# Gate-up chunks of three feed-forwards as seven quarter products over sums of quarters, tiles in three parts with own down products

## The chip, the cores and the metric

One core of one Trainium2 chip. The time is that of the program on the device in microseconds, taken as the median over runs; lower is better. TensorE is called PE, VectorE DVE, ScalarE ACT, GpSimd POOL, SyncE SP, as in the profile.

## What is computed

The program is two blocks of a language model over 512 tokens with 1024 features, in 32-bit floats: pooling, sparse attention and a short convolution in the first (with 16 more tokens ahead), two kinds of attention in the second, and three feed-forwards. Only these matter here:

```python
gate, up = jnp.split(hn @ w_gate_up, 2, axis=-1)
h = h + (jax.nn.silu(gate) * up) @ w_down
...
x = x + 0.5 * swiglu(rms_norm_2(x, ffn1_norm[i]), ffn1_w_gate[i], ffn1_w_up[i], ffn1_w_down[i])
...
x = x + 0.5 * swiglu(rms_norm_2(x, ffn2_norm[i]), ffn2_w_gate[i], ffn2_w_up[i], ffn2_w_down[i])
```

Each has 2816 hidden features, which are 22 tiles of 128 (`FK`).

## The kernel before

The residual `hT` lies transposed in SBUF: eight tiles (k = 0 to 7) of 128 features by 16 + 512 tokens. Weights come in numbered chunks of 128 x 2048 floats (1 MB, two transfers of 512 KB). A chunk c goes through four stages, with two buffers each, chosen by c % 2:

- SP loads it into `raw` (`load`, line 394), once POOL is done with chunk c - 2.
- ACT rounds it to PE's 32-bit format into `whi` (`high`, line 1206) once PE is done with chunk c - 2.
- POOL subtracts, `wlo = raw - whi`, in four parts (`low`, line 566).
- PE multiplies. A product of full precision is three passes: high weights by high activations, high by low, low by high (`passes`, lines 693 to 695). `chunk` makes two output tiles (t = 0, 1) of 128 x 512 tokens, each over eight k: 48 matmuls of 512 columns. The outputs lie in two of eight PSUM banks, chosen by c % 2, and PE waits on `acc_free` until they have been read.

In a feed-forward (f = 0, 1, 2, each engine has its function `ffn`) the chunks C_F[f] + n hold gate tile n and up tile n. PE sums the squares during the first chunk, ACT takes the root, DVE the reciprocal `rs` (line 1705), which ends during the second chunk. In the second feed-forward two norms follow each other, and DVE and ACT take turns twice (`closing_root`). For tile n DVE scales gate and up by `rs` into `tmp` (line 1736), ACT takes the silu (line 1251), DVE multiplies (line 1761), ACT rounds the product to `fh` (line 1253), DVE makes its low part `fl` (line 1764). ACT's order for tile n is: `high` of chunk n + 2, silu of tile n, rounding of tile n.

When all 22 tiles are there, 12 down chunks follow: four blocks of 256 output features, each in three chunks of 8, 8 and 6 tiles of k that add up in one PSUM bank, so that DVE adds a block to `hT` once, after its third chunk (`update`). Each finished tile is fed on (`feed`): ACT scales and rounds it to `xh` and squares it, DVE makes `xl` and adds the squares, for the next stage. In the second feed-forward DVE scales the eight tiles of `hT` (line 1677 of the profile) ahead of its down chunks.

The order of work is the order of each engine's code: engines run theirs strictly in turn and wait on semaphores. Gate-up and down chunks were loops on every engine; the second attention's chunks are written out.

## Time and profile before

| | |
|---|---|
| median of 3 runs | 1999.79 us (1999.69 to 2000.12) |
| span of the profiled execution | 1998.1 us |
| the profiled execution's own time | not given apart; the median has 1.7 us around the span |
| PE busy | 1990.9 us, 9505 matmuls |
| POOL, DVE, ACT busy | 1007.5, 877.9, 732.3 us |
| feed-forwards in the span | about 487 to 846, 846 to 1219 and 1580 to 1938 us |
| mean HBM traffic | 92 GB/s |

The profile has one execution. Busy time of PE is modelled and overlaps, so that the distance between starts is the price of a matmul, not its duration. A wait is put down to what ended it.

### The profile page before, as it was taken

What the parts mean: (1) busy time and instruction counts of PE and PEld (TensorE: products, weight loads), DVE (VectorE), ACT (ScalarE), POOL (GpSimd) and SP (SyncE); (2) the same over time, 40 slices, a digit from 0 to 9 for tenths busy, and PEclk for the clock granted to TensorE, in tenths of its full rate; (3) what the DMA queues carried; (4) which work ended last, traced back from release to release, by engine and by line L of the source; (5) the groups of instructions that cost most, each with busy time, mean ns of one, the idle gap of its engine ahead of it and who ended that gap; (6) DMA issues with size and microseconds to landing.
All of it is one profiled execution on the core that took longest, in us unless ns stands there. A gap on an engine that the chain in (4) does not pass through costs nothing.

```text
span 1998.1 us, 26696 instructions
## 1 busy us (share of the span) xinstructions
PE 1990.9 (100%) x9505; PEld 1668.7 (84%) x9505; DVE 877.9 (44%) x1467; ACT 732.3 (37%) x1034; POOL 1007.5 (50%) x795
## 2 busy tenths in 40 slices
PE   9999999999999999999999999999999999999999
PEld 8998887788888888888888888889888888888887
DVE  6587756535333322153334115677645523332124
ACT  6413234444222323232232225667643422322232
POOL 5444442245555544455555446565654555555443
PEclk9999999999999999999999999999999999999999
DMA  5233231133333332333332232332222333332332
GB/s 179 87 92 99 85 104 43 49 100 93 96 105 86 103 100 80 109 90 105 85 104 90 98 107 85 109 103 75 72 87 85 104 105 84 105 95 89 98 107 85
DMA packets 253787, 188.81 MB, mean 94 GB/s; under 512 B 6608, under 2 KB 249680, under 8 KB 253680
## 3 DMA queue, kind: packets, MB, share of 16 engines
q1 hardware_dynamic: 253024, 187.53, 31.5%
q8 instruction: 44, 0.72, 0.2%
q10 hardware_dynamic: 688, 0.31, 0.1%
q14 instruction: 31, 0.25, 0.0%
HBM read 180.93 MB, written 2.10 MB: 92 GB/s over the span
## 4 chain that ended last, share of the span: by engine, by line
PE 98%; ACT 1%; DVE 1%; issue 0%; DMA 0%; SPq 0%; ACTq 0%; DVEq 0%
PE ps L693 30%; PE ps L695 30%; PE ps L694 30%; PE ps L989 1%; PE ps L1141 1%; PE ps L1061 1%; PE ps L1062 1%; PE ps L1063 1%; PE ps L1129 1%; PE ps L1128 0%; PE ps L983 0%; PE ps L1111 0%; PE ps L1099 0%; PE ps L882 0%; PE ps L1098 0%
## 5 line engine op out<-in xcount | busy, mean ns | idle before, releaser
L566 POOL TENSOR_TENSOR wlo<-raw,whi 128x512 fp32r<-128x512 f32 (+2 forms) x636 | 852.9, 1373 | 862.1 <-ACT whi L1206 773.1
L693 PE MATMUL ps<-xh,whi 128*128 128x512 f32 (+1 forms) x1872 | 716.1, 383 | 0.0
L695 PE MATMUL ps<-xh,wlo 128*128 128x512 f32 (+1 forms) x1872 | 709.0, 379 | 0.0
L694 PE MATMUL ps<-xl,whi 128*128 128x512 f32 (+1 forms) x1872 | 708.7, 379 | 0.0
L1206 ACT ACTIVATE whi<-raw 128x2048 fp32r<-128x2048 f32 (+1 forms) x149 | 280.1, 1880 | 765.0 <-PE ps L695 764.9
L695 PEld LDWEIGHTS ps<-xh,wlo 128*128 128x128 f32 x1872 | 351.5, 188 | 66.8
L693 PEld LDWEIGHTS ps<-xh,whi 128*128 128x128 f32 x1872 | 351.7, 188 | 64.4 <-issue 0.7
L694 PEld LDWEIGHTS ps<-xl,whi 128*128 128x128 f32 x1872 | 352.0, 188 | 62.1 <-issue 0.7
L1736 DVE TENSOR_TENSOR tmp<-ps,rs 128x512 f32<-128x512 f32 x148 | 101.9, 691 | 313.1 <-PE ps L695 295.6
L695 PE MATMUL ps<-fh,wlo 128*128 128x512 f32 x528 | 205.4, 389 | 0.0
L693 PE MATMUL ps<-fh,whi 128*128 128x512 f32 x528 | 205.4, 389 | 0.0
L694 PE MATMUL ps<-fl,whi 128*128 128x512 f32 x528 | 205.4, 389 | 0.0
L1677 DVE SCALAR_TENSOR_TENSOR hT<-ps,hT 128x512 f32 x40 | 27.6, 690 | 270.6 <-PE ps L695 269.6
L1761 DVE TENSOR_TENSOR tmp<-tmp 128x512 f32<-128x512 f32 x66 | 90.3, 1369 | 111.9 <-ACT tmp L1251 111.7
L693 PEld LDWEIGHTS ps<-fh,whi 128*128 128x128 f32 x528 | 99.1, 188 | 20.7
L694 PEld LDWEIGHTS ps<-fl,whi 128*128 128x128 f32 x528 | 99.1, 188 | 20.6
L695 PEld LDWEIGHTS ps<-fh,wlo 128*128 128x128 f32 x528 | 99.1, 188 | 20.5
L644 POOL TENSOR_TENSOR wlo<-raw,whi 128x384 fp32r<-128x384 f32 (+1 forms) x84 | 75.6, 931 | 51.3 <-ACT whi L1572 50.6
L1211 ACT ACTIVATE xh<-hT,vec (+1 forms) x48 | 34.9, 727 | 127.2 <-DVE hT L1677 125.7
L1253 ACT ACTIVATE fh<-tmp 128x512 f32 x66 | 41.8, 633 | 102.4 <-DVE tmp L1761 102.4
L1764 DVE TENSOR_TENSOR fl<-tmp,fh 128x512 f32 x66 | 51.2, 775 | 62.3 <-ACT fh L1253 62.3
L1677 DVE SCALAR_TENSOR_TENSOR xl<-hT,vec,xh (+1 forms) x48 | 46.0, 960 | 57.5 <-ACT xh L1211 57.4
(335 smaller groups left out, 2247.1 us busy)
## 6 DMA issues: line engine op xcount, KB each, us to landing
raw<-in_w_in SPq DMA_DIRECT2D x87, 512.0 KB, 4.6
raw<-in_w_gate_up SPq DMA_DIRECT2D x44, 512.0 KB, 4.7
raw<-in_ffn_w_gate SPq DMA_DIRECT2D x44, 512.0 KB, 4.0
raw<-in_ffn_w_up SPq DMA_DIRECT2D x44, 512.0 KB, 5.2
raw<-in_ffn_w_down SPq DMA_DIRECT2D x32, 512.0 KB, 4.0
raw<-in_w_down SPq DMA_DIRECT2D x16, 512.0 KB, 4.0
raw<-in_ffn_w_down SPq DMA_DIRECT2D x16, 384.0 KB, 3.6
raw<-in_w_b SPq DMA_DIRECT2D x8, 512.0 KB, 4.0
```

The lines of the kernel that those rows point to most:

```text
L566: ins = pool.tensor_tensor(wlo[:, c % 2, cs], raw[:, c % 2, cs], whi[:, c % 2, cs].bitcast(F32), ALU.subtract)
L644: ins = pool.tensor_tensor(wlo[:, c % 2, cs], raw[:, c % 2, cs], whi[:, c % 2, cs].bitcast(F32), ALU.subtract)
L693: pe.matmul(o, w_of(whi), xhi, start=first, stop=False)
L694: pe.matmul(o, w_of(whi), xlo, start=False, stop=False)
L695: return pe.matmul(o, w_of(wlo), xhi, start=False, stop=last)
L1206: act.activation(whi[:, c % 2, 0:n], raw[:, c % 2, 0:n], ACT.Copy).then_inc(w_hi, 1)
L1211: act.activation(one(xh, nn)[:, lo:TM], one(hT, nn)[:, lo:TM], ACT.Copy, scale=col(vec, lin(gain + n, per, i))).then_inc(xh_done, 1)
L1253: act.activation(one(fh, lin(n, per, i)), tmp[:, 3, :], ACT.Copy).then_inc(h_hi, 1)
L1677: return dve.scalar_tensor_tensor(o, a, s, b, op0, op1)
L1736: dve.tensor_tensor(o, ps[0:o.shape[0], bank(c, t), :], rsx[0:o.shape[0]], ALU.mult).then_inc(acc_free, 1)
L1761: dve.tensor_tensor(tmp[:, 3, :], tmp[:, 1, :], tmp[:, 2, :], ALU.mult).then_inc(h_done, 1)
L1764: dve.tensor_tensor(one(fl, nn), tmp[:, 3, :], one(fh, nn).bitcast(F32), ALU.subtract).then_inc(h_split, 1)
```

## The change

Of the 22 tiles of a feed-forward, 18 (tiles 4 to 21) are *folded*. The weights of a chunk are taken as four corners (k 0 to 3 or 4 to 7, gate or up) of 512 x 128, and the tokens as two halves, early and late, of 256. Instead of eight products of a corner with a quarter of the activations, each engine's code makes seven, over sums of corners and sums of activation quarters (the scheme of Strassen and Winograd): 7 x 4 k x 3 passes = 84 matmuls of 256 columns. Sums of weights: DVE forms three in PSUM (`corner_sums`), ACT rounds them, DVE makes their low parts (`sums_low`); POOL forms the fourth (`low_sum`) and the low parts of three corners. Sums of activations (`fold_forms`, `fold_sums`: "forms" below, numbers 0 to 3) are made once per feed-forward, by ACT and DVE together, number 0 at place 0, numbers 1 and 2 at place 1, number 3 at place 2. Three partial products are copied out of PSUM by ACT (`kept`) and added by DVE; PE goes on with the bank when the copy is made. The low part of an activation moves from DVE to POOL (`act_low`).

A feed-forward has 34 *places* p, chunk C_F[f] + p: 7 up tiles, 4 down chunks over tiles 0 to 5, 8 up tiles, 4 down chunks over tiles 6 to 13, 7 up tiles, 4 down chunks over tiles 14 to 21. `fh` and `fl` are rings of nine tiles. Each down chunk has its own PSUM bank per half and is added to `hT` by DVE in two steps. Silu and product of a tile now run at the place after it. All loops of the feed-forwards are written out. Some semaphores are merged and buffers moved, in stages that stay as they are.

Core of the diff (`corner_sums`, `sums_low` and `act_low` are told above):

```diff
-DOWN_K = (8, 8, 6)
+DOWN_K = (6, 8, 8)
+UPS = (7, 8, 7)
+PLAIN = 4
+RING = 9
+FOLD = CW
...
+FORMS_AT = {0: (0,), 1: (1, 2), 2: (3,)}
...
+            def fold_low(f, p):
+                c, n = C_F[f] + p, fold_no(f, p)
+                for z, (a, b) in enumerate(((0, 0), (1, 1), (1, 0))):
+                    hi, lo = unit(c, z)
+                    if z == 2:
+                        pool.wait_ge(w_lo, c)
+                        pool.tensor_tensor(low_sum[:], corner(c, 1, 1), corner(c, 0, 1), ALU.subtract).then_inc(corner_low, 1)
+                    pool.wait_ge(raw_hi, 3 * n + z + 1)
+                    pool.tensor_tensor(by_k(lo), corner(c, a, b), by_k(hi).bitcast(F32), ALU.subtract).then_inc(raw_lo, 1)
+                if up_tile(p - 2) is not None:
+                    act_low(f, p - 2)
+                hi, lo = unit(c, 3)
+                pool.wait_ge(w_hi, c + 1)
+                pool.tensor_tensor(by_k(lo), low_sum[:], by_k(hi).bitcast(F32), ALU.subtract).then_inc(w_lo, 1)
...
+            def ffn(f):
+                low(C_F[f])
+                low(C_F[f] + 1)
+                for p in range(1, FFN_LEN):
+                    if folded(p + 1):
+                        fold_low(f, p + 1)
+                        continue
+                    if down_part(p) is not None and up_tile(p - 1) is not None:
+                        act_low(f, p - 1)
+                    if p + 1 < FFN_LEN:
+                        low(C_F[f] + p + 1)
+                    if down_part(p) is None and up_tile(p - 1) is not None:
+                        act_low(f, p - 1)
...
+                pe.wait_ge(raw_lo, 3 * n + 1)
+                pe.wait_ge(acc_free, 2 * (c - 2) + 2)
+                product(r1, 0, xh[:, k1, late], xl[:, k1, late]).then_inc(prod_done, 1)
+                if n % (FK - PLAIN) == 0:
+                    pe.wait_ge(fs_lo, 8 * f + 8)
+                pe.wait_ge(sum_lo, 3 * n + 1)
+                product(r5, 4, *forms(0)).then_inc(prod_done, 1)
+                pe.wait_ge(sum_lo, 3 * n + 2)
+                pe.wait_ge(prod_kept, 3 * n + 1)
+                product(r1, 5, *forms(2), first=False).then_inc(prod_done, 1)
+                pe.wait_ge(raw_lo, 3 * n + 2)
+                pe.wait_ge(prod_kept, 3 * n + 2)
+                product(r5, 1, *forms(3), first=False).then_inc(prod_done, 1)
+                pe.wait_ge(w_lo, c + 1)
+                pe.wait_ge(prod_kept, 3 * n + 3)
+                product(r1, 3, *forms(1), first=False).then_inc(prod_done, 1)
+                pe.wait_ge(raw_lo, 3 * n + 3)
+                pe.wait_ge(up_done, 2 * n + 1)
+                product(r2, 2, xh[:, k2, late], xl[:, k2, late]).then_inc(tile_done, 1)
+                pe.wait_ge(sum_lo, 3 * n + 3)
+                pe.wait_ge(up_done, 2 * n + 2)
+                product(r1, 6, xh[:, k2, early], xl[:, k2, early], first=False).then_inc(tile_done, 1)
...
+                pe.wait_ge(w_lo, c + 1)
+                for t in range(2):
+                    pe.wait_ge(acc_free, 2 * (c - 2) + t + 1)
+                    for k in range(DOWN_K[r]):
+                        if j == 0 and t == 0:
+                            pe.wait_ge(h_split, FK * f + k0 + k + 1)
+                        o, z = CW * k + P * t, (k0 + k) % RING
+                        mm = passes(ps[:, bank(c, t), :], c % 2, lambda wt: wt[:, c % 2, o:o + P],
+                                    fh[:, z, :], fl[:, z, :], k == 0, k == DOWN_K[r] - 1)
+                    mm.then_inc(tile_done, 1)
...
-                def up(c, n, per=0, i=None):
-                    high(c + 2, per, i)
-                    act.wait_ge(acc_free, lin(2 * c + 1, 2 * per, i))
-                    act.activation(tmp[:, 1, :], tmp[:, 0, :], ACT.Silu).then_inc(silu_done, 1)
-                    act.wait_ge(h_done, lin(FK * f + n + 1, per, i))
-                    act.activation(one(fh, lin(n, per, i)), tmp[:, 3, :], ACT.Copy).then_inc(h_hi, 1)
...
+            def fold_high(f, p, z):
+                c, n = C_F[f] + p, fold_no(f, p)
+                def corner_high(u, a, b):
+                    act.activation(by_k(unit(c, u)[0]), corner(c, a, b), ACT.Copy).then_inc(raw_hi, 1)
+                def sum_high(u, m):
+                    act.wait_ge(corner_sum, 3 * n + min(m + 2, 3))
+                    act.activation(unit(c, u)[0], ps[:, 3 + 2 * m, :], ACT.Copy).then_inc(sum_hi, 1)
+                if z == 0:
+                    act.wait_ge(raw_in[c % 2], raw_level(c, 0, None))
+                    if n:
+                        act.wait_ge(corner_sum, 3 * n - 2)
+                    act.activation(sums(1), corner(c, 0, 1), ACT.Copy).then_inc(corner_in, 1)
+                    act.wait_ge(tile_done, 2 * (c - 1))
+                    corner_high(0, 0, 0)
+                elif z == 1:
+                    corner_high(1, 1, 1)
+                    sum_high(4, 0)
+                elif z == 2:
+                    sum_high(5, 1)
+                else:
+                    corner_high(2, 1, 0)
+                    sum_high(6, 2)
+                    act.wait_ge(corner_low, n + 1)
+                    act.activation(by_k(unit(c, 3)[0]), low_sum[:], ACT.Copy).then_inc(w_hi, 1)
...
+            def fold_forms(f, i, gain):
+                for z, n in enumerate((i, i + 4)):
+                    ins = act.activation(ps[:, 1, FOLD * z:FOLD * z + FOLD], hT[:, n, META:META + FOLD], ACT.Copy,
+                                         scale=vec[:, gain + n:gain + n + 1])
+                ins.then_inc(fs_in, 1)
+                for z in range(2):
+                    act.wait_ge(fs_sum, 2 * (4 * f + i) + z + 1)
+                    act.activation(fsh[:, 2 * z:2 * z + 2, i, :], ps[:, 5 + 2 * z, :].rearrange("p (y t) -> p y t", y=2),
+                                   ACT.Copy).then_inc(fs_hi, 1)
...
+                act.wait_ge(rt_done, S + 1)
+                for p in range(FFN_LEN):
+                    c, n = C_F[f] + p, up_tile(p - 1)
+                    def coming(z):
+                        if folded(p + 1):
+                            fold_high(f, p + 1, z)
+                        elif folded(p):
+                            high_piece(c + 1, z)
+                        elif p and z == 0:
+                            high(c + 1)
+                    def kept(dst, src, level):
+                        if folded(p):
+                            act.wait_ge(prod_done, 5 * fold_no(f, p) + level)
+                            act.activation(dst[:], src, ACT.Copy).then_inc(prod_kept, 1)
+                    r1, r5, _ = fold_out(c)
+                    if n is not None and not folded(p - 1):
+                        act.wait_ge(acc_free, 2 * (c - 1) + 1)
+                        act.activation(tmp[:, 1, :], tmp[:, 0, :], ACT.Silu).then_inc(silu_done, 1)
+                    for i in FORMS_AT.get(p, ()):
+                        fold_forms(f, i, own)
+                    coming(0)
+                    if folded(p - 1):
+                        act.wait_ge(acc_free, 2 * c)
+                        act.activation(tmp[:, 1, :], tmp[:, 0, :], ACT.Silu).then_inc(silu_done, 1)
+                    kept(prod1, r1, 1)
+                    coming(1)
+                    kept(prod5, r5, 2)
+                    coming(2)
+                    if n is not None:
+                        act.wait_ge(h_done, FK * f + n + 1)
+                        act.activation(fh[:, n % RING, :], tmp[:, 3, :], ACT.Copy).then_inc(h_hi, 1)
+                    kept(prod6, r1, 3)
+                    coming(3)
...
+            def fold_sums(f, i, own):
+                a, b = slice(0, FOLD), slice(FOLD, T)
+                early, late = slice(META, META + FOLD), slice(META + FOLD, TM)
+                x, s13, s24 = ps[:, 1, :], ps[:, 5, :], ps[:, 7, :]
+                g1, g2 = (vec[:, own + n:own + n + 1] for n in (i, i + 4))
+                dve.wait_ge(fs_in, 4 * f + i + 1)
+                if f or i:
+                    dve.wait_ge(fs_lo, 2 * (4 * f + i))
+                link(stt(s13[:, a], hT[:, i, early], g1, x[:, b], ALU.mult, ALU.add))
+                stt(s13[:, b], hT[:, i, late], g1, x[:, a], ALU.mult, ALU.subtract)
+                stt(s24[:, a], hT[:, i, late], g1, s13[:, a], ALU.mult, ALU.subtract).then_inc(fs_sum, 1)
+                dve.wait_ge(fs_sum, 2 * (4 * f + i) + 1)
+                stt(s24[:, b], hT[:, i + 4, late], g2, s24[:, a], ALU.mult, ALU.add).then_inc(fs_sum, 1)
+                for z, s in enumerate((s13, s24)):
+                    dve.wait_ge(fs_hi, 2 * (4 * f + i) + z + 1)
+                    dve.tensor_tensor(fsl[:, 2 * z:2 * z + 2, i, :], s.rearrange("p (y t) -> p y t", y=2),
+                                      fsh[:, 2 * z:2 * z + 2, i, :].bitcast(F32), ALU.subtract).then_inc(fs_lo, 1)
...
+                for p in range(FFN_LEN):
+                    c, n, last = C_F[f] + p, up_tile(p - 1), FK * f + (up_tile(p - 1) or 0)
+                    new = folded(p + 1)
+                    if folded(p - 1):
+                        done(c - 1, 1)
+                        dve.tensor_tensor(tmp[:, 0, 0:FOLD], fold_out(c - 1)[0], rsx[:, 0:FOLD], ALU.mult).then_inc(acc_free, 1)
+                    if new:
+                        corner_sums(f, p + 1, 0)
+                        corner_sums(f, p + 1, 1)
+                    if n is not None:
+                        dve.wait_ge(silu_done, last + 1)
+                        if last:
+                            dve.wait_ge(h_split, last)
+                        if folded(p - 1):
+                            dve.wait_ge(up_done, 2 * fold_no(f, p - 1) + 2)
+                            dve.tensor_tensor(tmp[:, 3, :], tmp[:, 1, :], tmp[:, 2, :], ALU.mult).then_inc(h_done, 1)
+                        else:
+                            done(c - 1, 1)
+                            link(dve.tensor_tensor(tmp[:, 3, :], tmp[:, 1, :], ps[:, bank(c - 1, 1), :], ALU.mult))
+                            dve.sem_inc(acc_free, 1)
+                            dve.sem_inc(h_done, 1)
+                    for i in FORMS_AT.get(p, ()):
+                        fold_sums(f, i, own)
+                    if new:
+                        corner_sums(f, p + 1, 2)
+                        sums_low(f, p + 1, 0)
+                        sums_low(f, p + 1, 1)
+                    if folded(p):
+                        m = fold_no(f, p)
+                        r1, r5, r2 = fold_out(c)
+                        dve.wait_ge(prod_done, 5 * m + 4)
+                        dve.wait_ge(prod_kept, 3 * m + 3)
+                        dve.wait_ge(h_done, FK * f + up_tile(p))
+                        dve.tensor_tensor(tmp[:, 2, FOLD:T], r5, prod6[:], ALU.add).then_inc(up_done, 1)
...
+                        stt(tmp[:, 2, :], ps[:, bank(c, t), :], factor, rsx, ALU.mult, ALU.mult).then_inc(acc_free, 1)
+                        dve.wait_ge(acc_free, 2 * c + t + 1)
+                        dve.tensor_tensor(x, x, tmp[:, 2, :], ALU.add).then_inc(h_new, 1)
```

## Rows read from the trace of the kernel before

**Rows 1.** The page: busy time and share of each engine; the chain that ended last, by engine.
```profile
PE 1990.9 (100%) x9505; PEld 1668.7 (84%) x9505; DVE 877.9 (44%) x1467; ACT 732.3 (37%) x1034; POOL 1007.5 (50%) x795
...
PE 98%; ACT 1%; DVE 1%; issue 0%; DMA 0%; SPq 0%; ACTq 0%; DVEq 0%
```

**Rows 2.** Timeline at the third gate-up chunk: start us, duration us, engine, line, operation.
```profile
508.65 0.39 PE L693 MATMUL ps<-xh,whi 128*128 128x512 f32 x1
...
508.85 1.92 ACT L1206 ACTIVATE whi<-raw 128x2048 fp32r<-128x2048 f32 x1 [4.74 <-PE ps L695]
...
519.73 1.92 ACT L1206 ACTIVATE whi<-raw 128x2048 fp32r<-128x2048 f32 x1 [6.28 <-PE ps L695]
```

**Rows 3.** Timeline of PE in a value chunk with 256 columns.
```profile
1363.75 0.28 PE L1061 MATMUL ps<-whi,xh 128*128 128x256 f32 x1
...
1364.71 0.28 PE L1063 MATMUL ps<-whi,xl 128*128 128x256 f32 x1
```

**Rows 4.** Matmuls of the output projection's first pass: duration ns min/median/max, first and last start.
```profile
L693 PE MATMUL ps<-mh,whi x64: 389/389/389, 442.9 to 485.8; 128*128 128x512 f32 x64
```

**Rows 5.** Groups of ACT and DVE by shape: count, busy us, mean ns, idle before.
```profile
L1253 ACT ACTIVATE fh<-tmp 128x512 f32 x66 | 41.8, 633 | 102.4 <-DVE tmp L1761 102.4
...
L1416 ACT ACTIVATE fpTh<-ps 128x256 fp32r<-128x256 f32 x16 | 6.2, 384 | 17.8 <-PE ps L1129 17.7
...
L1736 DVE TENSOR_TENSOR tmp<-ps,rs 128x512 f32<-128x512 f32 x148 | 101.9, 691 | 313.1 <-PE ps L695 295.6 <-DVE fl L1764 12.5 <-DVE rs L1705 0.4
L1761 DVE TENSOR_TENSOR tmp<-tmp 128x512 f32<-128x512 f32 x66 | 90.3, 1369 | 111.9 <-ACT tmp L1251 111.7
...
L2174 DVE TENSOR_TENSOR fpTl<-ps,fpTh 128x256 fp32r<-128x256 f32 x16 | 6.8, 422 | 5.4 <-ACT fpTh L1416 5.3
```

**Rows 6.** Groups of POOL by shape.
```profile
L566 POOL TENSOR_TENSOR wlo<-raw,whi 128x512 fp32r<-128x512 f32 x556 | 781.9, 1438 | 752.9 <-ACT whi L1206 735.5 <-ACT whi L1346 17.4
...
L566 POOL TENSOR_TENSOR wlo<-raw,whi 128x384 fp32r<-128x384 f32 x48 | 47.4, 1021 | 37.6 <-ACT whi L1206 37.6
```

**Rows 7.** Timeline of POOL: one part beside a DVE op, one alone.
```profile
512.10 1.74 POOL L566 TENSOR_TENSOR wlo<-raw,whi 128x512 fp32r<-128x512 f32 x1
...
1593.30 1.29 POOL L566 TENSOR_TENSOR wlo<-raw,whi 128x512 fp32r<-128x512 f32 x1 [3.80 <-ACT whi L1206]
```

**Rows 8.** Timeline at the start of the first feed-forward: ACT's rounding, DVE after the root.
```profile
497.97 1.92 ACT L1206 ACTIVATE whi<-raw 128x2048 fp32r<-128x2048 f32 x1
...
500.19 1.29 DVE L1736 TENSOR_TENSOR tmp<-ps,rs 128x512 f32<-128x512 f32 x2 [0.22 <-DVE rs L1705]
```

**Rows 9.** The same at the second and third feed-forward.
```profile
863.04 1.72 DVE L1724 TENSOR_TENSOR rs<-rs,ssum 128x512 f32<-128x512 f32 x1
864.98 1.29 DVE L1736 TENSOR_TENSOR tmp<-ps,rs 128x512 f32<-128x512 f32 x2 [0.22 <-DVE rs L1724]
...
869.71 1.92 ACT L1206 ACTIVATE whi<-raw 128x2048 fp32r<-128x2048 f32 x1 [1.24 <-PE ps L695]
...
1591.30 1.92 ACT L1206 ACTIVATE whi<-raw 128x2048 fp32r<-128x2048 f32 x1 [1.41 <-PE ps L695]
...
1592.20 1.29 DVE L1736 TENSOR_TENSOR tmp<-ps,rs 128x512 f32<-128x512 f32 x2 [0.22 <-DVE rs L1705]
```

**Rows 10.** Timeline of PE at the start of the kernel.
```profile
1.07 4.51 PE L743 MATMUL ps<-ones 128*128 128x512 f32 x10 [1.07 <-DVE eps L1801]
```

**Rows 11.** Timeline of DVE: the eight scalings ahead of the second down stage.
```profile
1093.07 7.15 DVE L1677 SCALAR_TENSOR_TENSOR hT<-hT,vec,ssum 128x512 f32<-128x512 f32 x8 [0.22 <-DVE fl L1764]
```

**Rows 12.** Timeline of POOL and DVE at the last chunk of a projection.
```profile
1573.40 5.49 POOL L566 TENSOR_TENSOR wlo<-raw,whi 128x512 fp32r<-128x512 f32 x4 [5.47 <-ACT whi L1206]
...
1580.12 0.69 DVE L1677 SCALAR_TENSOR_TENSOR hT<-ps,hT 128x512 f32 x1 [0.68 <-PE ps L695]
```

**Rows 13.** Page, DMA issues: count, KB each, us to landing.
```profile
raw<-in_ffn_w_up SPq DMA_DIRECT2D x44, 512.0 KB, 5.2
```

**Rows 14.** Busy time of each engine in the unrolled attention stage, granted clock, DMA.
```profile
1280.00:1492.00 212.00, 211.36 (x1177) 183.34 (x1176) 136.26 (x306) 133.24 (x299) 123.09 (x123) 1.00 0.33 95
```

More of the change, by code:

```diff
@@ L322, in n_cols @@
                 return DK * (P + KW)
[L323 to L326 removed]
+            part = down_part(ffn_place(c)[1])
+            return CH if part is None else DOWN_K[part[0]] * CW
         def value_tile(c, t, z):
```

341 lines of the change are left out of this document (203 added, 138 removed).

## Prediction

> **What bounds the kernel now.** I read the page's busy times first, then the chain that ended last, then the timeline of single chunks. TensorE (PE) is busy for 1990.9 of 1998.1 us, and the chain is PE for 98% [rows 1]: what shortens the work of PE shortens the kernel, as long as nothing else makes PE wait. The stretch of the feed-forwards has the shape to remember. ScalarE (ACT) starts its rounding of a weight chunk 0.20 us after PE begins the chunk before it (508.65 to 508.85), and the next one comes 10.88 us later [rows 2]. So one gate-up chunk is 48 matmuls of 512 columns at 0.2267 us, with no hole. Behind it run ACT (1.92 us to round), then POOL (four low parts, 5.2 to 5.9 us): some 8 us of each 10.88. That chain is hidden, but it has under 3 us to spare: an ACT that comes to its rounding late shows at once.
>
> **1. The seven products.** A folded chunk issues 7 products x 4 k x 3 passes = 84 matmuls of 256 columns. The nearest rows are the value chunks with 256 columns: eight steps in 0.96 us, 0.120 us each [rows 3]. 84 x 0.120 = 10.08 against 10.88 us: 0.80 us less. 54 chunks are folded (18 in each of three feed-forwards): **-43.2 us**. The bounds: half of 0.2267 (0.113 us) would give 1.36 us a chunk, -73; 0.122 us, -34. I take the row, which has the shape itself. The 12 waits within a chunk cost nothing once they are met: the output projection waits ahead of each of its k, and its 64 first passes, three matmuls apart, take 42.9 us, 0.681 a step, three times 0.227 [rows 4].
> The Trainium skill (TensorE: Matmul & The Clock Gate, section Back-to-back issue gap) has a smaller fixed part per matmul, 2.5 ns beside the columns; by it the chunks would be 10.36 and 9.17 us and the term -64. Rows 2 and 3 give more than that at both widths, and the rows decide.
>
> **2. The steady folded chunk.** What is prepared for the next chunk while PE works on this one, in us from PE's start, with 0.19 for PE's last result to reach another engine: ACT has eight copies of 512 (six halves and sums rounded, one corner into PSUM, one sum of POOL's), three of 256, a silu and a rounding: 10 x 0.63 + 3 x 0.38 = 7.4 of 10.08. DVE has six of 512 with a PSUM operand, five of 256 and the product of the silu: 6 x 0.69 + 5 x 0.42 + 1.37 = 7.6. POOL has six of 512 (before four; the activation's low part moves to it): 8.6 at the mean of 1.438, 7.7 at the 1.29 of an undisturbed one [rows 5 to 7]. All fit. The tightest hand-off is the third product, which ACT must copy out (0.38) before PE's fifth writes there at 5.76. Ahead of it ACT has a corner (to 0.82), the silu (1.34), the first copy (2.05), a corner and a sum (3.1), the second copy (3.5), the second sum, which waits for DVE's third corner sum (4.15), and the rounding of the activation (4.7); the copy ends at 5.0. Slack 0.75: nothing is paid. The fifth product's sum on DVE ends at 7.8, needed at 8.64. **0 us**, with up to 0.1 late (5 us in all) if no ACT copy overlapped the next and DVE's product took its full 1.37.
>
> **3. The start of each feed-forward.** This is where I expect the loss. Chunk 2 (the third) needs its weights rounded by ACT. Before, ACT did that ahead of the silu, at 497.97, right after the table load [rows 8]. Now ACT's order at place 1 is: silu of tile 0, forms 1, forms 2, and only then the rounding of chunk 2. The silu waits for DVE's scaling of tile 0, which stands behind the root (its reciprocal; tmp is written from 500.19 [rows 8]) and behind forms 0. From the root's end R, with 0.04 a hand-off:
> - forms 0: four 256-wide sums on DVE, 0.42 each with hand-offs between (1.85), ACT's copy of the last (0.63), DVE's low part (0.69): the scaling starts at R + 3.3
> - scaling 0.69, silu 0.63, product 0.69: R + 5.4
> - forms 1: 1.85 + 0.63, and ACT's two scaled halves for forms 2 (0.75): R + 8.7; forms 2: 1.85 + 0.63: R + 11.2
> - rounding 1.92, started 0.1 before the copy's end as ACT's ops do, four parts on POOL at 1.29: **R + 18.2**.
> R is 500.19; PE wants chunk 2 at 508.65 [rows 2]: it waits 9.7 us. In the second feed-forward R was 864.98, of which 1.03 is a product that ran 1.72 instead of 0.69 beside POOL, which now stands still; chunk 2 was due 0.20 before 869.71: 863.95 + 18.2 - 869.51 = 12.6. In the third, R 1592.20, due at 1591.10 + 10.88 = 1601.98: 8.4 [rows 9]. Sum **+30.8**. The bounds: 0.69 for each of the 12 narrow sums adds 12 x 0.27 x 3 = +10; if they overlap throughout and the POOL parts follow faster, -9.
> **The clock.** After such a wait PE may come back at its lower level. The only row of that is the kernel's start: ten 512-column matmuls take 4.51 us, 0.45 apart and not 0.227, while the column of the granted clock shows full speed there too; 2.2 us are lost [rows 10]. Without it, chunk 3 would come 0.7 late in its turn (forms 3 stand ahead of its rounding, 4.5 + 1.9 + 5.2 = 11.6 from the start of chunk 2, against 10.88). One takes the place of the other: 0.7 to 2.2, I take 2.2 as the one with a row. **+6.6**.
>
> **4. From up to down.** The chunk after the last up tile is rounded in four pieces between ACT's other copies, the last ending at 5.5, and POOL's four parts end at 10.7 where PE wants them at 10.08: +0.65 in parts 1 and 2. In part 0 the down chunk has six k, POOL takes 4 x 1.02 and is in time [rows 6], but then the low part of tile 6 stands ahead of the next chunk's on POOL: ready at 8.9 after the first down chunk's start, wanted at 8.16: +0.75. Tile 21 is wanted 21 matmuls (4.76) into its down chunk and is ready 5.4 after the up chunk, 4.75 into it: nothing. 2.05 a feed-forward; in the second the eight scalings of the residual (7.15 us on DVE, two operands in SBUF each [rows 11]) now fall beside POOL's work for part 0: five POOL ops, slowed by some 0.35 each (an undisturbed one takes 1.29, the disturbed one of rows 7 1.74), 1.7 more. **+7.9**.
>
> **5. Down products alone.** Matmuls are the same in number. Each of 36 chunks has its own evacuation, per half one DVE pass from PSUM and one add: 4 us of 8.16 or more, covered by the next chunk, as PSUM has two sets. In the last part ACT's rounding stands behind the feed, 0.7 later than in the output projection, where POOL's four parts end at 1578.89 and the next chunk starts 0.19 before 1580.12, 1.04 later [rows 12]: 0.3 is left, covered; 0.3 is lost before the second feed-forward's sums of squares. **+0.3**. SP's loads are the same in number and size; a slot is freed at 9.5, filled 5.2 us later [rows 13] at 4.6 of the next chunk, and wanted at 6.5. Unrolled code: in the stretch that is unrolled now, PE stood 0.64 of 212 us [rows 14]; 0 to 3 us for the feed-forwards, taken as 0.
>
> **Sum.** -43.2 + 30.8 + 6.6 + 7.9 + 0.3 = +2.4 on a span of 1998.1; with the 1.7 us that the median of the runs (1999.8) has around it: **2002.2 us**.
>
> **The rivals.**
> (a) *The start is covered* (DVE and ACT get through the forms so early that chunk 2 is in time, or I have the order of waits wrong): the terms of 3 go, 2002.2 - 37.4 = 1965. For: ACT stands idle for most of the first chunks. Against: it stands idle waiting for the root, and so would the forms. In between, each microsecond off the chain R + 18.2 is 3 us.
> (b) *POOL becomes the bound*, slower than before. Six subtractions at 1.74 us, as the row of one that met a DVE op with two SBUF inputs [rows 7], are 10.44 us; over 10.08 by 0.36, times 54 is 19.4: 2021. It decides once the six, with POOL's waits for ACT (about 1.3 us), pass 10.08, that is from 1.46 us each. For: their mean in the feed-forwards is 1.438. Against: DVE now has one op a chunk with two SBUF inputs instead of two, since the sums lie in PSUM. The Trainium skill (SBUF — State Buffer, section Who interferes with whom) says that only such DVE ops hold GpSimd up. By that rule five of six run at 1.29, and this rival falls; the rows of 1.29 and 1.74 bear it out.
> (c) *The 256-column matmuls run at a worse pitch in this mix*: at 0.125 the 54 chunks take 84 x 0.005 x 54 = 23 us more: 2025. Against: rows 3.
>
> **How the numbers follow.** My case, 0.60, lies from 1990 to 2013 (chain -9 to +10, clock -4.5, code +3). (a) with its halfway forms 0.18, (b) 0.15, (c) 0.07. The range 1983 to 2021 leaves out most of (a) and the worst of (b) and (c). 0.2% is 4.0 us, about what a measurement of this kernel tells from no change: faster (below 1995.8) is (a) and the low fifth of my case, 0.32; slower (above 2003.8) is (b), (c) and a good third of mine, 0.42; the rest 0.26.
>
> **What would show it.** A folded chunk 10.08 us apart in the timeline. PE idle once per feed-forward ahead of chunk 2 for 8 to 13 us, released by POOL's low part, with ACT's copies of the forms before its rounding; matmuls 0.43 apart after it. Idle of about 0.7 before down chunks. I am wrong in step 2 if PE waits for ACT's copies within folded chunks, and in step 3 if PE runs through.

## The result, and the profile after

The changed kernel takes **2016.94 us** (median of 4 runs, 2016.16 to 2017.48), the kernel before 1999.82 beside it: 1.0085 times as long, 95% interval 1.0071 to 1.0099. It is slower by 17.1 us, and by more than the 2.4 us forecast; it lies inside the range of 1983 to 2021, but above the 1990 to 2013 of my own case. The profiled execution took 2016.82 us with a span of 2015.0.

The page of the changed kernel: busy times, the granted clock in 40 slices of the span, the chain by engine, and, by shape, two groups of POOL.

```profile
PE 1962.6 (97%) x11449; PEld 1731.6 (86%) x11449; DVE 1189.4 (59%) x2067; ACT 937.5 (47%) x1649; POOL 1123.3 (56%) x915
...
PEclk9999999999899999989999999999999989999999
...
PE 86%; DVE 4%; POOL 4%; ACT 4%; issue 2%; DMA 0%; SPq 0%; DVEq 0%; ACTq 0%
...
L631 POOL TENSOR_TENSOR wlo<-raw,whi 128x512 fp32r<-128x512 f32 x340 | 462.9, 1393 | 470.0 <-ACT whi L1350 414.9 <-ACT whi L1395 37.7 <-ACT whi L1561 17.5
...
L654 POOL TENSOR_TENSOR wlo<-raw,whi 128x512 fp32r<-128x512 f32 x162 | 212.9, 1316 | 160.1 <-ACT whi L1404 160.1
```

Beside [rows 1], PE's work has shrunk and the span has grown. The chain, 98% PE before, now leaves PE for a seventh of the span: something makes PE wait. POOL, the second rival's suspect, is no busier than 56%, and its subtractions of 512 columns have become shorter: 1.393 us, and 1.316 in the folded chunks, where 1.438 stood in [rows 6]. The clock column has a dip in slices 11, 18 and 33, where the feed-forwards begin. The list of PE's waits (us in total, how many, the longest) says who ends them:

```profile
PE ps L793 <- POOL wlo L631: 40.8, 15, 12.7
PE ps L944 <- ACT prod L1461: 4.7, 6, 0.8
```

For a ledger I took, from 480 us on, every distance from the start of a matmul of 512 or 256 columns to the next start, and subtracted what the shape takes undisturbed: 0.2267 us for 512 columns [rows 2], 0.120 for 256 [rows 3]. What is left over, called lost below, adds up to 6.7 us before and 67.2 after. So 60.5 us are lost and 43.2 won, which is the 17. Where the clock stays full, a loss is 0.2 to 0.3 us more than the idle time in brackets, since the first matmuls behind a wait are further apart. Where they are lost:

| place | f = 0 | f = 1 | f = 2 | sum | forecast |
|---|---|---|---|---|---|
| ahead of chunk 2, slow clock included | 12.84 | 14.70 | 10.54 | 38.1 | 37.4 |
| ahead of the second down chunk of part 0 | 1.33 | 4.70 | 1.33 | 7.4 | 4.0 |
| ahead of the first down chunk of parts 1 and 2 | 1.26 | 1.26 | 1.25 | 3.8 | 3.9 |
| ahead of the fourth product of the first folded chunk of parts 1 and 2 | 2.04 | 2.02 | 2.04 | 6.1 | 0 |
| chunks of the last part's feed | 3.73 | 0.1 | 0.1 | 3.9 | 0.3 |

The folded chunks themselves run as fast as forecast. PE at the first chunk and at the end of the third of a row:

```profile
543.00 0.28 PE L944 MATMUL ps<-xh,whi 128*128 128x256 f32 x1
543.11 0.28 PE L945 MATMUL ps<-xl,whi 128*128 128x256 f32 x1
...
573.11 0.28 PE L946 MATMUL ps<-xh,foldl 128*128 128x256 f32 x1
573.23 0.40 PE L793 MATMUL ps<-fh,whi 128*128 128x512 f32 x1
```

From 543.00 to 573.23 are three chunks of 84 matmuls, 30.23 us: 10.08 each.

The start of the first feed-forward, PE (in brackets the idle time before an instruction, and who ended it):

```profile
508.15 0.39 PE L795 MATMUL ps<-xh,wlo 128*128 128x512 f32 x1
518.28 0.79 PE L793 MATMUL ps<-xh,whi 128*128 128x512 f32 x1 [9.74 <-POOL wlo L631]
518.87 0.63 PE L794 MATMUL ps<-xl,whi 128*128 128x512 f32 x1
519.30 0.63 PE L795 MATMUL ps<-xh,wlo 128*128 128x512 f32 x1
...
523.99 0.57 PE L794 MATMUL ps<-xl,whi 128*128 128x512 f32 x1
524.39 0.39 PE L795 MATMUL ps<-xh,wlo 128*128 128x512 f32 x1
```

And ACT there:

```profile
501.17 1.12 ACT L1436 ACTIVATE fsh<-ps 128x512 fp32r<-128x512 f32 x2 [2.67 <-DVE ps L1892]
503.73 0.63 ACT L1466 ACTIVATE tmp<-tmp 128x512 f32<-128x512 f32 x1 [1.43 <-DVE tmp L2057]
504.26 0.86 ACT L1431 ACTIVATE ps<-hT,vec 128x256 f32<-128x256 f32 x2
506.83 1.12 ACT L1436 ACTIVATE fsh<-ps 128x512 fp32r<-128x512 f32 x2 [1.72 <-DVE ps L1892]
507.85 0.87 ACT L1431 ACTIVATE ps<-hT,vec 128x256 f32<-128x256 f32 x2
510.30 1.12 ACT L1436 ACTIVATE fsh<-ps 128x512 fp32r<-128x512 f32 x2 [1.57 <-DVE ps L1892]
511.32 1.90 ACT L1350 ACTIVATE whi<-raw 128x2048 fp32r<-128x2048 f32 x1
```

PE stands 9.74 us for POOL, and POOL began its four parts at 513.30, when ACT had rounded. ACT rounds at 511.32, behind the silu (503.73), forms 1 and forms 2; before, it did that ahead of the silu [rows 8]. In between it stands idle three times for DVE (1.43, 1.72, 1.57 us), with the rounding ready to run. After the wait, matmuls start 0.427 us apart.

### The profile page after: what moved, and what is told of

It is laid out like the page before. It is cut to its first block, busy times and chain, and to the rows that moved or that the text cites. A ratio compares the mean times of both kernels' runs of the same rounds, so it can differ in the third digit from the quotient of the medians.

```text
span 2015.0 us, 30682 instructions
## 1 busy us (share of the span) xinstructions
PE 1962.6 (97%) x11449; PEld 1731.6 (86%) x11449; DVE 1189.4 (59%) x2067; ACT 937.5 (47%) x1649; POOL 1123.3 (56%) x915
## 3 DMA queue, kind: packets, MB, share of 16 engines
q8 instruction: 87, 1.43, 0.3%
## 4 chain that ended last, share of the span: by engine, by line
PE 86%; DVE 4%; POOL 4%; ACT 4%; issue 2%; DMA 0%; SPq 0%; DVEq 0%; ACTq 0%
PE ps L793 18%; PE ps L794 18%; PE ps L795 18%; PE ps L944 8%; PE ps L946 8%; PE ps L945 8%; POOL wlo L631 4%; PE ps L1133 1%; PE ps L1285 1%; ACT whi L1350 1%; DVE ps L1892 1%; PE ps L1205 1%; PE ps L1206 1%; PE ps L1207 1%; DVE tmp L1892 1%
## 5 line engine op out<-in xcount | busy, mean ns | idle before, releaser
L631 POOL TENSOR_TENSOR wlo<-raw,whi 128x512 fp32r<-128x512 f32 (+2 forms) x420 | 537.5, 1312 | 579.1 <-ACT whi L1350 433.9
L793 PE MATMUL ps<-xh,whi 128*128 128x512 f32 (+1 forms) x1008 | 383.5, 380 | 31.7 <-POOL wlo L631 31.7
L794 PE MATMUL ps<-xl,whi 128*128 128x512 f32 (+1 forms) x1008 | 375.2, 372 | 0.0
L795 PE MATMUL ps<-xh,wlo 128*128 128x512 f32 (+1 forms) x1008 | 375.1, 372 | 0.0
L654 POOL TENSOR_TENSOR wlo<-raw,whi 128x512 fp32r<-128x512 f32 x162 | 212.9, 1316 | 160.1 <-ACT whi L1404 160.1
L793 PEld LDWEIGHTS ps<-xh,whi 128*128 128x128 f32 x1008 | 191.2, 190 | 65.0 <-POOL wlo L631 33.8
L795 PEld LDWEIGHTS ps<-xh,wlo 128*128 128x128 f32 x1008 | 190.8, 189 | 33.7
L794 PEld LDWEIGHTS ps<-xl,whi 128*128 128x128 f32 x1008 | 191.5, 190 | 28.9 <-issue 0.7
L944 PE MATMUL ps<-fsh,whi 128*128 128x256 f32 x432 | 122.7, 284 | 4.7 <-ACT prod L1461 4.7
L946 PE MATMUL ps<-xh,wlo 128*128 128x256 f32 x432 | 122.3, 283 | 0.0
```

The lines of the kernel that those rows point to most:

```text
L631: ins = pool.tensor_tensor(wlo[:, c % 2, cs], raw[:, c % 2, cs], whi[:, c % 2, cs].bitcast(F32), ALU.subtract)
L654: pool.tensor_tensor(by_k(lo), corner(c, a, b), by_k(hi).bitcast(F32), ALU.subtract).then_inc(raw_lo, 1)
L793: pe.matmul(o, w_of(whi), xhi, start=first, stop=False)
L794: pe.matmul(o, w_of(whi), xlo, start=False, stop=False)
L795: return pe.matmul(o, w_of(wlo), xhi, start=False, stop=last)
L944: pe.matmul(o, wh[:, ks], hi[:, k, :], start=first and k == 0, stop=False, skip_group_check=True)
```

## The experiments

Each kernel is the changed one with one thing altered; the last ones put several together. Times beside 2016.94. The start in the wanted order and the last two kernels were run 4, 5 and 5 times, each of the others once.

### ACT rounds before it makes the forms

```diff
+                    coming(0)
                     for i in FORMS_AT.get(p, ()):
                         fold_forms(f, i, own)
-                    coming(0)
```

> ACT rounds the next chunk's weights ahead of the forms at places 1 and 2, nothing else is changed. Theory (the rounding of chunk 2 waits in ACT's order behind forms 1 and 2, and POOL and PE with it): the rounding of chunk 2 starts some 6.5 us earlier, right behind the silu of tile 0, and the three waits of 9.7, 12.7 and 8.4 us ahead of chunk 2 shrink by 6 to 7 us each, to about 3, 6 and 2. With the clock's loss unchanged the kernel takes 1995 to 1998 us, and 1990 where the clock no longer falls. First rival (DVE's reciprocal and forms, not ACT's order, set the start): the waits stay within 1 us of what they were, 2015 us or more. Second rival (the forms are wanted just as much): as much is lost again ahead of chunk 4, the first folded one, by PE waiting for the low parts of the forms, and the time stays at 2012 or more.

Measured: 1991.53 us. One line moved, 25.4 us less. The list of PE's waits:

```profile
PE ps L793 <- POOL wlo L631: 19.7, 15, 5.6
```

21.1 us of waits are gone (40.8 to 19.7), and the three starts lose 3.0, 7.4 and 1.7 us in the ledger. The first rival falls: DVE's forms are as they were. So does the second: no new wait for the forms. In the second feed-forward the clock still falls; the 1995 to 1998 and the 1990 of the theory were for all three places or none, and it came out between.

### Forms 2 one place later

```diff
-    FORMS_AT = {0: (0,), 1: (1, 2), 2: (3,)}
+    FORMS_AT = {0: (0,), 1: (1,), 2: (2, 3)}
```

> Forms 2 are made at place 2 together with forms 3, in place of place 1. Theory (ACT's order, and one op of it is worth what it takes): the wait ahead of chunk 2 is shorter by what forms 2 take, 2.5 to 2.9 us in each feed-forward; forms 2 and 3 then stand ahead of the rounding of chunk 3, behind a product of DVE's that waits for POOL's low part of tile 0, and chunk 3 comes 2 to 4 us late in its turn. The sum is within 4 us of 2016.8. Rival (forms 2 have room at place 2): the first wait is shorter and none appears, 2008 us.

Measured: 2013.21 us. PE's idle times ahead of chunk 2 are 6.28, 9.18 and 4.97 us, each 3.5 shorter, not 2.5 to 2.9: forms 2 take ACT from 507.85 to 511.32 above, 3.5. With the slow clock behind them the starts lose 8.0, 11.6 and 6.8 us, 11.7 less in all. And chunk 3 is late by 4.5, 2.2 and 2.7 us, 9.4 together. The wait moves, as expected: what stands ahead of a rounding is paid at one chunk or at the next. Of the 3.7 us that the kernel is faster, 1.6 lie elsewhere: at the second down chunk of part 0 in the second feed-forward PE stands the same 2.83 us, but the clock does not fall behind it, and 3.1 us are lost and not 4.7.

### PE kept busy through the wait

```diff
+                        if p == 2:
+                            for _ in range((40, 52, 34)[f]):
+                                pe.matmul(ps[:, 3, :], ones[:], xh[:, 0, META:TM], start=True, stop=True)
                         chunk(c + p, xh, xl)
```

> PE makes 40, 52 and 34 matmuls of 512 columns with no use ahead of chunk 2 of the three feed-forwards (9.1, 11.8 and 7.7 us at 0.227 each, a little less than its waits there), into a PSUM bank that holds nothing at that time. Theory (the 0.43 us from one matmul to the next behind the wait come from PE having stood still): with them the matmuls of chunk 2 are 0.227 apart from the first on, the remaining wait is under 1 us in each, and 6 to 8 us are won: 2009 to 2011 us. The granted clock's half level is gone from these three places. Rival (the slow matmuls come from chunk 2's own data or from POOL and ACT beside them): the pitch behind the wait stays at 0.43 and the time at 2016 to 2018.

Measured: 2013.52 us, 3.4 less and not 6 to 8. PE where the useless matmuls end and chunk 2 begins:

```profile
516.17 1.29 PE L1002 MATMUL ps<-xh,ones 128*128 128x512 f32 x5
518.26 0.50 PE L793 MATMUL ps<-xh,whi 128*128 128x512 f32 x1 [0.79 <-POOL wlo L631]
518.59 0.40 PE L794 MATMUL ps<-xl,whi 128*128 128x512 f32 x1
518.83 0.39 PE L795 MATMUL ps<-xh,wlo 128*128 128x512 f32 x1
```

The mechanism is as the theory has it: the first two distances are 0.33 and 0.24, then 0.23, and the three starts, with 28.6 us of useless matmuls counted as wait, lose 32.0 in place of 38.1. So the slow clock costs 6.1 us at the three starts. But now chunk 3 is late: 0.93, 0.93 and 0.85 us, 2.7 together. While PE was slow, POOL caught up. Net 3.4, which is the difference in time. The prediction had this ("Without it, chunk 3 would come 0.7 late in its turn"); my expectation for this run had forgotten it.

### ACT's start in the order in which it is wanted

```diff
 # fold_forms, between its scalings and its copies
+                if i == 0:
+                    high(C_F[f] + 2)
 # ffn: the first two tiles rounded ahead of the forms, chunk 3 after forms 1
+                    if p in (1, 2):
+                        act.wait_ge(h_done, FK * f + n + 1)
+                        act.activation(fh[:, n % RING, :], tmp[:, 3, :], ACT.Copy).then_inc(h_hi, 1)
                     for i in FORMS_AT.get(p, ()):
                         fold_forms(f, i, own)
+                        if i == 1:
+                            high(C_F[f] + 3)
```

> ACT's work at the start of a feed-forward is put in the order in which it is wanted: it rounds chunk 2 right after its first two scalings for forms 0, while DVE makes them; chunk 3 after forms 1; and the products of tiles 0 and 1 ahead of the forms of their places. Theory (all 38 us lost at the three starts, clock included, come from ACT's order): the waits ahead of chunks 2 go to under 1.5 us in the first and third feed-forward and under 3 in the second, none larger than 1 us comes ahead of chunks 3 and 4, and the kernel takes 1978 to 1985 us, faster than the kernel before. First rival (only the order is changed, and DVE's forms are late for chunk 4 instead): a wait of 3 us or more for the forms ahead of its second product, 1990 or more. Second rival (the loss is spread over all folded chunks and not at the starts): 2005 or more.

Measured: **1983.72 us** (1983.34 to 1984.75), 0.992 times the kernel before, interval 0.9903 to 0.9936. ACT at the start:

```profile
498.72 0.88 ACT L1431 ACTIVATE ps<-hT,vec 128x256 f32<-128x256 f32 x2
499.53 1.90 ACT L1350 ACTIVATE whi<-raw 128x2048 fp32r<-128x2048 f32 x1
502.27 1.12 ACT L1438 ACTIVATE fsh<-ps 128x512 fp32r<-128x512 f32 x2 [0.83 <-DVE ps L1899]
```

The rounding fits into the 2.67 us for which ACT stood idle ahead of 501.17. In the first and third feed-forward the starts lose nothing at chunks 2 and 3, and 0.5 and 0.2 us at the first folded chunk. In the second they lose 4.1 there:

```profile
889.66 0.28 PE L946 MATMUL ps<-fsh,foldl 128*128 128x256 f32 x1
892.38 0.55 PE L944 MATMUL ps<-fsh,foldh 128*128 128x256 f32 x1 [2.44 <-ACT prod L1463]
892.73 0.42 PE L945 MATMUL ps<-fsl,foldh 128*128 128x256 f32 x1
```

That is more than the theory's 1 us ahead of chunk 4, and it is the first rival's place, though for a product's copy and not for the forms. The root comes later there, two norms in a row [rows 9]: the forms begin 5.7 us before PE starts chunk 2 (859.38 and 865.12), in the first feed-forward 8.6 (500.83 and 509.47), and all that follows them is late.

### POOL's order at the first down chunk

```diff
-                    if down_part(p) is not None and up_tile(p - 1) is not None:
+                    if down_part(p) == (2, 0):
                         act_low(f, p - 1)
                     if p + 1 < FFN_LEN:
                         low(C_F[f] + p + 1)
-                    if down_part(p) is None and up_tile(p - 1) is not None:
+                    if down_part(p) != (2, 0) and up_tile(p - 1) is not None:
                         act_low(f, p - 1)
 # PE's down_chunk
-                    pe.wait_ge(acc_free, 2 * (c - 2) + t + 1)
+                    pe.wait_ge(acc_free, 2 * (c - 2) + (2 if folded(p - 2) else t + 1))
```

> POOL makes the low part of the last up tile of parts 0 and 1 (which the down products of the part don't use) behind the four low parts of the next down chunk, not ahead of them; PE's first half of the second down chunk waits for both halves of the folded chunk before. Theory (the second down chunk of part 0 is late by the one POOL op that stands ahead of its low parts): PE's losses there, 1.33, 4.70 and 1.33 us after the change, go to 0.1, under 1.5 and 0.1, and the kernel takes 2009 to 2011 us. The losses of 0.63 ahead of the first down chunk of parts 1 and 2 stay. Rival (POOL is late by the residual's scalings beside it in the second feed-forward, not by its order): the 1.33 go and of the 4.70 at least 2.5 stay, 2011 to 2014. Second rival (ACT's rounding is late, not POOL's part): nothing moves, 2016 to 2018.

Measured: 2010.89 us, 6.0 less. The losses of 1.33, 4.70 and 1.33 us are gone, the second one whole. POOL in the changed kernel in the first feed-forward, and below in the second:

```profile
576.96 1.29 POOL L643 TENSOR_TENSOR fl<-tmp,fh 128x512 fp32r<-128x512 f32 x1 [3.24 <-ACT fh L1479]
578.21 4.37 POOL L631 TENSOR_TENSOR wlo<-raw,whi 128x384 fp32r<-128x384 f32 x4
...
946.83 1.73 POOL L643 TENSOR_TENSOR fl<-tmp,fh 128x512 fp32r<-128x512 f32 x1 [3.25 <-ACT fh L1479]
948.52 8.53 POOL L631 TENSOR_TENSOR wlo<-raw,whi 128x384 fp32r<-128x384 f32 x6
```

Here POOL in this experiment:

```profile
575.29 4.85 POOL L631 TENSOR_TENSOR wlo<-raw,whi 128x384 fp32r<-128x384 f32 x4 [1.34 <-ACT whi L1350]
580.10 1.28 POOL L643 TENSOR_TENSOR fl<-tmp,fh 128x512 fp32r<-128x512 f32 x1
```

POOL had stood 3.24 us for ACT's rounding of tile 6, with the chunk's parts behind it; now they start 2.9 us earlier and the tile's low part fills the time after. The rival with the residual's scalings names a true slowing, but one that decides only while POOL's order makes the chunk late at all.

### DVE's second addition after the corner sums

```diff
 # place of the last down chunk of parts 0 and 1
+                        if t and j == 3 and r < 2:
+                            continue
 # the place after it
                         corner_sums(f, p + 1, 2)
+                        if down_part(p) is None and down_part(p - 1) is not None:
+                            add_down(c - 1, down_part(p - 1)[0], 3, 1)
```

> At the end of parts 0 and 1 DVE adds the second half of the last down chunk to the residual only after the third corner sum of the next place, not before that place. Theory (the first folded chunk of a part waits for ACT's copy of a product because DVE's two additions, two SBUF inputs each, stand ahead of its corner sums, for which ACT waits ahead of that copy): the six losses of 1.08 and 0.96 us at the third product of that chunk go to under 0.2, and the kernel takes 2010 to 2012 us. Rival (ACT is simply full there, with its rounding in pieces or a weight chunk that has come late): the six losses stay, 2016 to 2018.

Measured: 2012.39 us, 4.5 less. The loss lies ahead of the chunk's fourth product, which waits for ACT's copy of the second; the expectation counts it as the third. Changed kernel, DVE and then ACT at the first folded chunk of part 1:

```profile
609.25 0.85 DVE L2079 TENSOR_TENSOR hT<-hT,tmp 128x512 f32<-128x512 f32 x1
610.02 0.69 DVE L1989 TENSOR_TENSOR ps<-ps,raw 128x512 f32<-128x512 f32 x1
610.81 0.70 DVE L1992 TENSOR_TENSOR ps<-ps,raw 128x512 f32<-128x512 f32 x1
...
611.55 0.60 ACT L1408 ACTIVATE foldh<-ps 128x512 fp32r<-128x512 f32 x1 [1.76 <-DVE ps L1992]
612.04 0.38 ACT L1461 ACTIVATE prod<-ps 128x256 f32<-128x256 f32 x1
```

This experiment, ACT:

```profile
609.35 0.60 ACT L1408 ACTIVATE foldh<-ps 128x512 fp32r<-128x512 f32 x1
609.84 0.38 ACT L1461 ACTIVATE prod<-ps 128x256 f32<-128x256 f32 x1
```

ACT no longer stands 1.76 us for DVE, the copy of the product comes 1.7 us earlier (2.2 by the numbers, and this run lies 0.5 earlier as a whole), and PE's six losses, 6.1 us, are gone. Three of 0.27 are new, where the addition now delays DVE's sum with the fourth product, for which the sixth waits. That ACT is full there, the rival, is refuted: it was idle.

### The feed's odd tile after the rounding

```diff
-                        for t in range(2):
-                            m = 2 * down_part(p)[1] + t
+                        m0 = 2 * down_part(p)[1]
+                        for m in range(max(m0 - 1, 0), m0 + (2 if m0 == 6 else 1)):
```

> In the down chunks of the last part ACT feeds the odd tile of a pair only after the rounding of the next chunk. Theory (the losses of 1.50, 1.11 and 1.12 us at the last down chunks of the first feed-forward, whose feed squares each tile twice, come from ACT's rounding behind two whole feeds): they go to under 0.3 and the kernel takes 2012 to 2014 us; the second and third feed-forward, which lose 0.1 there, don't change. Rival (DVE's sum of squares is what comes late, and its order is unchanged): they stay, 2016 to 2018, or 1 us comes in front of the sums of squares of the second feed-forward.

Measured: 2013.68 us, 3.3 less. The losses of 1.50, 1.11 and 1.12 us are under 0.05 each, and no wait comes ahead of the sums of squares. The theory holds.

### The pieces one step earlier

```diff
-                            high_piece(c + 1, z)
+                            for y in ((0,), (1, 2), (3,), ())[z]:
+                                high_piece(c + 1, y)
```

> The four pieces in which ACT rounds the first down chunk of a part come one step earlier among its other copies: one, then two, then one, none at the end. Theory (POOL's four low parts start with the last piece, 0.6 us too late): the six losses of 0.63 us ahead of the first down chunk of parts 1 and 2 go to under 0.1, part 0 does not change, and the kernel takes 2012.5 to 2014 us. Rival (earlier pieces push ACT's copies of the products back, and PE waits for those in the same chunk): up to 0.7 us comes at the third or fifth product of the nine last folded chunks of a part, 2015 to 2020.

Measured: 2016.34 us, 0.6 less. The six losses of 0.63 us are gone and none comes within the folded chunks, so the theory has its place right and the rival falls. But in part 2 PE now stands for tile 21:

```profile
PE ps L793 <- POOL fl L643: 1.7, 3, 0.6
```

0.83 us in place of 0.2 in each feed-forward: PE is 0.63 earlier, and tile 21 is ready no earlier. In part 1, where the down chunk does not use the newest tile, 1.9 us should stay, but 0.16 comes anew ahead of the second down chunk in each feed-forward, which leaves 1.4. One run shows 0.6 of them, beside starts that vary by 1 us; so this order's worth alone is not shown.

### All five orders together, and tile 21 last

> The five orders together: the start as in e4, POOL's as in e5, DVE's as in e6, the feed as in e7, the pieces as in e8. Theory (the losses are separate, and the seven products bring 43.2 us): from the 1983.7 of e4 go the 7.3 us of the second down chunks of part 0, 5.3 at the third products, 3.3 at the feed and 1.9 at the first down chunks: 1966 us, between 1963 and 1970, 1.6 to 1.8% faster than the kernel before. Rival (the orders get in each other's way: an engine that is moved forward in one place holds up another in the next): 1972 or more, with a wait of PE of over 1 us at a place where no single change had one.

Measured: **1964.93 us** (1964.17 to 1965.21, 5 runs), **0.9824** times the kernel before, interval 0.9810 to 0.9837. It beats both kernels. The first lines of its waits:

```profile
PE ps L944 <- ACT prod L1464: 3.1, 3, 2.4
PE ps L793 <- POOL fl L643: 1.6, 3, 0.6
```

The ledger has 14.8 us left, 8.1 over that of before; -43.2 + 8.1 = -35.1, and the measured difference is -35.2. So the seven products bring what they were forecast to bring. That the losses are separate is borne out by the forecast of 1966 from the single changes, and no wait over 1 us is new. One by one the five orders saved 33.2, 6.0, 4.5, 3.3 and 0.6 us, 47.6 in all, and together 52.0. Some 2 us of the 4.4 between them lie in the single runs, whose three starts together lose 0.1 to 1.2 us more than the changed kernel's; the rest I have not traced. Nearly half of what is left is the first folded chunk of the second feed-forward (3.6 us); I did not try to mend that.

The next one changes PE's order in the first down chunk of part 2, on top of the five:

```diff
+                order = [(t, k) for t in range(2) for k in range(DOWN_K[r])]
+                if r == 2 and j == 0:
+                    order = [(t, k) for t in range(2) for k in range(7)] + [(0, 7), (1, 7)]
```

> As e9, and in the first down chunk of part 2 PE takes tile 21, which comes last, at the end of both output tiles, not at the end of the first. Theory (PE waits there for POOL's low part of tile 21, 0.83 us in each feed-forward since the pieces come earlier): these three waits go, 2.5 us, and the kernel takes 2 to 3 us less than e9, some 1963.5. Rival (the next chunk is then as late by the same amount, since its buffers come free later): the time is within 1 us of e9's.

Measured: 1965.40 us (1964.72 to 1965.61), no gain. The three waits for tile 21 are gone, 2.5 us. In the first feed-forward, whose feed is the longest, PE loses 0.6 and 1.5 us anew, the first ahead of the third down chunk of the part, the second within the next feed-forward's first chunk, where it waits for the last tile fed:

```profile
839.86 0.50 PE L793 MATMUL ps<-xh,whi 128*128 128x512 f32 x1 [1.27 <-DVE xl L1904]
```

The first output tile of the down chunk with the new order is finished later, and so is the feed behind it: ACT begins it at 801.19, in the kernel with the five orders at 797.11. The rival is right in effect for that feed-forward, though PE waits behind the feed and not for buffers, and wrong for the other two.

## Why the prediction was right, and where it was not

**Step 1, the seven products, -43.2.** Right: 10.08 us a chunk, 54 times, and the ledger of the five orders together, where -43.2 and the losses left make up the difference. The rows of before decided, and after bears them out. The Trainium skill (TensorE: Matmul & The Clock Gate, section Back-to-back issue gap) gives the formula behind my -64 for an isolated matmul, which I had not said; for a stream of weight loads and matmuls it has about 131 ns at 512 columns, and the trace has 227 here.

**Step 2, the steady chunk, 0.** Right for 48 of 54 chunks: within them PE has no gap over 0.05 us. It failed at the first folded chunk of parts 1 and 2: **6.1 us where I had none**. The step sorted ACT's and DVE's work of a steady chunk, which has a folded one before it. Behind a down chunk DVE comes from two evacuations whose additions have two operands in SBUF, and its first corner sum starts at 610.02, 1.7 us later than without the second of them; the 0.75 us of slack that I had counted for ACT's third copy did not matter, since the second one was late. The experiment with DVE's order shows it.

**Step 3, the start, +37.4.** Right in mechanism, place and size: 38.1. The waits were to be 9.7, 12.6 and 8.4; the trace has 9.74 and 12.66 at the first two, and 8.4 at the third. The chain from the root's end, R = 499.73, to PE at 518.28 is 18.55 us and was to be 18.2; forms 0 took 3.28 (3.3), forms 2 3.5 (2.5, with scalings already made). That the first wait came out to 0.04 us is luck in part: the root was ready 0.46 us earlier than I had it, and the chain is 0.35 longer. The clock was to cost 6.6 and costs 6.1, and it takes the place of chunk 3's lateness, as said (0.7 each forecast, 0.9 once PE is kept busy). That the cause is ACT's order is shown by the one line moved, and by the start in the wanted order.

**Step 4, from up to down, +7.9.** Nearly right: 0.63 lost (0.65) in parts 1 and 2, and in part 0 PE stood 1.05 and lost 1.33 (0.75). In the second feed-forward it stood 2.83, so 1.8 longer (1.7), with POOL beside the scalings of the residual:

```profile
946.00 10.18 DVE L1892 SCALAR_TENSOR_TENSOR hT<-hT,vec,ssum 128x512 f32<-128x512 f32 x8
```

They took 7.15 alone [rows 11] and take 10.18 beside POOL, whose low part of a tile takes 1.73 and not 1.29. By the Trainium skill (SBUF — State Buffer, section Who interferes with whom) a DVE instruction with two SBUF inputs contends with a GpSimd instruction that reads SBUF; the trace agrees, and shows both sides slower. What I left out is that the clock falls after this wait as well: with it 4.70 us are lost, 1.9 more than PE stood. Measured 11.2 in place of 7.9.

**Step 5, down products alone, +0.3.** Wrong by 3.6 us: I had 0.7 late and 1.04 in hand, from a feed of one square. In the first feed-forward each tile is squared twice, ACT has 0.6 us more per tile, and three chunks are late by 1.1 to 1.5. ACT's order is not all of it. POOL at a chunk's four low parts in the last part, in the first and in the third feed-forward:

```profile
834.23 6.37 POOL L631 TENSOR_TENSOR wlo<-raw,whi 128x512 fp32r<-128x512 f32 x4 [5.65 <-ACT whi L1350]
...
1939.12 5.93 POOL L631 TENSOR_TENSOR wlo<-raw,whi 128x512 fp32r<-128x512 f32 x4 [5.04 <-ACT whi L1350]
```

I had 5.49 [rows 12]. In the first feed-forward ACT's rounding starts 3.61 us after PE begins the chunk, in the third 2.89: 0.72 later; and POOL takes 0.44 longer, beside a second addition of squares on DVE. Together they are the 1.1 us.

**The sum.** Losses of 45.6 us were forecast and 60.5 came. The 14.9 between them (14.7 between the times, 2002.2 and 2016.9) are the wait ahead of the fourth products 6.1, the feed 3.6, step 4 3.3, the start 0.7, and 1.2 elsewhere, of which 0.6 are three waits for tile 21 that step 4 had at nothing. So the sum missed by 14.7 us and left the range of my own case, 1990 to 2013. The range given, to 2021, was so wide for the sake of rivals (b) and (c), and both fell: that the time lies in it is luck. All missed terms have one sign, for a reason: each is a place where a steady stretch meets another, and I had worked out the steady ones closely and looked at the joints only where the diff wrote something special. **The rivals:** (a), the covered start, was no description of this kernel, but of the start in the wanted order: it took 1983.7, 33.2 us less than the changed kernel, where (a) had valued it at 37.4. (b), POOL, fell: 1.316 us a subtraction, below the 1.46 from which it decides. I had also priced it too low: with its own 1.3 us of waits, six at 1.74 are 11.74 a chunk, 90 us over all chunks and not 19. (c), a worse pitch, fell as well: 0.120 us.

## What to carry to other kernels

Ahead of judging a change by what it saves, ask of each engine that runs in strict order what stands in front of the instruction that the next weights wait for. Here 52 of the 60 us lost went by order alone: five reorderings that remove no work turn 0.9% slower into 1.8% faster. Work that was moved off the bounding engine was free in the steady stretch and was paid at the joints: the start after a norm, up to down, down to up, the feed. And when a wait is removed, look who was catching up behind it.

## What the runs showed of the hardware

PE came back at the half level of the granted clock (0.50 in the profile, matmuls of 512 columns 0.427 us apart, of 256 columns 0.21) after it had stood 9.74, 12.66, 8.42 and 5.59 us, and the slow matmuls lasted 3 to 6 us. The fall lies within the wait: in the first, the granted clock is 1.00 from 508.6 to 510.6 us and 0.50 from 510.8 to 524.3. Waits of 2.4 to 2.9 us went either way. PE came back at full speed and kept it after 2.74 us (ACT rounding first) and after 2.40 (the five orders), and came back at the half level after 2.44 (the start in the wanted order). The wait of 2.83 in the second feed-forward was followed by the half level in the changed kernel, and by none in the kernel with forms 2 later. There PE also came back at full speed after 2.60, and fell to the half level 1.5 us later in the middle of the work:

```profile
529.94 0.50 PE L793 MATMUL ps<-xh,whi 128*128 128x512 f32 x1 [2.60 <-POOL wlo L631]
530.27 0.40 PE L794 MATMUL ps<-xl,whi 128*128 128x512 f32 x1
...
531.43 0.57 PE L793 MATMUL ps<-xh,whi 128*128 128x512 f32 x1
531.80 0.63 PE L794 MATMUL ps<-xl,whi 128*128 128x512 f32 x1
```

So the same wait of 2.83 us cost 4.70 in one kernel and 3.10 in another. The loss at a start varied by about 1 us from kernel to kernel at the same place (starts of the first feed-forward: 12.8, 12.6, 11.8, 11.5 and 12.7 us in the changed kernel and the four that leave its start alone), so that a gain of 1 us or less in one run of a kernel is not shown.
